# Experts' weighted rows added to their tokens in PSUM by matmuls with a selection matrix; norm read from there; pooling mixer in float32 with narrower tiles

## What is computed

```python
# first block: every token goes to 2 of 32 experts
expert = grp[:, None] * EXPERTS_PER_GROUP + top_i        # 2 per token
weights = softmax(top_v) * p_grp
for each expert e: y[e] = (silu(gate) * up) @ w_down[e]  # gate, up = split(x_rows @ w_gate_up[e])
y = zeros.at[tok_s].add(y_buf[dest] * w_s[:, None])      # weighted sum back onto the tokens
x = layer_norm(DN_ALPHA * x + y, ln2_g, ln2_b)
# second block: 16 meta tokens in front, L = 272
h = concat([meta, x]);  a = rmsnorm(h, norm_mix[0])
# pool_mixer: 4 groups of 256 columns, windows 2, 4, 8, 16 over the positions
pooled[g] = (cs - lag) / cnt - a[..., group g]
h = h + (pooled[g] @ pool_w[g]) * pool_scale
h = h + swiglu(rmsnorm(h, norm_ffn[0]), w_gate, w_up, w_down)   # then attention and a second FFN
```

## Time and profile before

| | |
|---|---|
| median of 3 runs | 1329.99 us (1329.01 to 1331.46) |
| the profiled execution, its own time | 1331.05 us |
| its span in the trace | 1329.8 us |
| PE busy | 1216.6 us (91%), weight loads 930.0 us |
| DVE busy | 545.1 us (41%) |
| ACT busy | 482.5 us (36%) |
| POOL busy | 158.2 us (12%) |
| moved by DMA | 337.38 MB, 253 GB/s read from HBM over the span |
| DMA on the SP queue | 321.46 MB, 64.1% of the 16 engines' time |

### The profile page before, as it was taken

One profiled execution on the slowest core, in us unless ns is written; L12 is line 12 of the kernel. 1 busy time (PEld: TensorE's weight loads), 2 busy tenths in 40 slices (PEclk: granted clock), 3 DMA queues, 4 the chain that ended last, 5 costly groups with the idle time before them and its releaser, 6 DMA issues. The chain is left out here.

```text
span 1329.8 us, 19383 instructions
## 1 busy us (share of the span) xinstructions
PE 1216.6 (91%) x8290; PEld 930.0 (70%) x8290; DVE 545.1 (41%) x646; ACT 482.5 (36%) x594; POOL 158.2 (12%) x169
## 2 busy tenths in 40 slices
PE   6999999899998888888877389999999999999998
PEld 6999889744433323232322279999999998999998
DVE  5665565600110001000001676665555436666643
ACT  6544663221211111111101544444346656544432
POOL 0630000002112010101000260000120000300011
PEclk9999999699999999999999589999999999999999
DMA  9743458399999999999997845544553233455530
GB/s 335 249 144 104 169 194 322 154 367 422 422 421 422 422 422 422 422 422 421 422 421 301 258 132 164 187 155 166 177 174 127 95 128 124 161 191 190 175 112 32
DMA packets 148949, 337.38 MB, mean 254 GB/s; under 512 B 7346, under 2 KB 118107, under 8 KB 124158
## 3 DMA queue, kind: packets, MB, share of 16 engines
q1 hardware_dynamic: 143280, 321.46, 64.1%
q0 software_dynamic: 3216, 9.44, 2.0%
q10 hardware_dynamic: 2366, 5.22, 1.1%
HBM read 329.79 MB, written 6.30 MB: 253 GB/s over the span
## 5 line engine op out<-in xcount | busy, mean ns | idle before, releaser
L1523 DVE TENSOR_TENSOR lo<-raw,hi 128x2048 fp32r<-128x2048 f32 (+1 forms) x112 | 251.3, 2247 | 154.0 <-ACT hi L1092 121.4
L1092 ACT CAST hi<-raw 128x2048 fp32r<-128x2048 f32 (+1 forms) x115 | 213.5, 1858 | 115.5 <-PE PS L432 96.0
L430 PE MATMUL PS<-AH,hi 128*128 128x272 f32 (+1 forms) x832 | 238.0, 286 | 2.5 <-DVE AL L1909 2.3
L432 PE MATMUL PS<-AH,lo 128*128 128x272 f32 (+1 forms) x832 | 237.3, 285 | 0.0
L431 PE MATMUL PS<-AL,hi 128*128 128x272 f32 (+1 forms) x832 | 237.0, 285 | 0.0
L430 PEld LDWEIGHTS PS<-AH,hi 128*128 128x128 f32 x832 | 156.9, 189 | 3.6 <-DVE AL L1909 2.9
L432 PEld LDWEIGHTS PS<-AH,lo 128*128 128x128 f32 x832 | 157.0, 189 | 0.0
L431 PEld LDWEIGHTS PS<-AL,hi 128*128 128x128 f32 x832 | 156.5, 188 | 0.1
L1870 DVE TENSOR_TENSOR HM<-T,PS 64x512 f32<-64x512 f32 x32 | 22.1, 690 | 313.8 <-ACT T L1278 313.8
L1278 ACT ACTIVATE T<-PS 64x512 f32<-64x512 f32 x32 | 18.9, 590 | 237.6 <-PE PS L702 237.6
L431 PE MATMUL PS<-FL,hi 128*128 128x272 f32 (+1 forms) x352 | 100.3, 285 | 0.0
(11 more groups left out here) (389 smaller groups left out, 2133.6 us busy)
## 6 DMA issues: line engine op xcount, KB each, us to landing
raw<-in_w_gate_up_dram SPq DMA_DIRECT2D x48, 1024.0 KB, 27.0
half<-in_w_gate_up_dram SPq DMA_DIRECT2D x45, 1024.0 KB, 27.7
spare<-in_w_gate_up_dram SPq DMA_DIRECT2D x35, 1024.0 KB, 27.0
half<-in_w_down_dram SPq DMA_DIRECT2D x26, 1024.0 KB, 28.0
raw<-in_w_down_dram SPq DMA_DIRECT2D x24, 1024.0 KB, 27.8
raw<-in_ffn_w_gate_dram SPq DMA_DIRECT2D x22, 1024.0 KB, 5.2
raw<-in_ffn_w_up_dram SPq DMA_DIRECT2D x22, 1024.0 KB, 5.3
raw<-in_w_in_dram SPq DMA_DIRECT2D x21, 1024.0 KB, 7.7
```

What stands on the lines that cost most here:

```text
L430: pe.matmul(o, w(h, c), xh(k), start=start and c == 0, stop=False)
L432: r = pe.matmul(o, w(l, c), xh(k), start=False, stop=stop and c == len(ks) - 1)
L1092: act.copy(K.view(K.hi[i % HN], 0, [[1, n]]), K.view(K.rbuf[i], 0, [[1, n]])).then_inc(S.hi, 1)
L1523: r = e.tensor_tensor(K.view(K.lo[i % HN], 0, [[1, n]]), K.view(K.rbuf[i], 0, [[1, n]]), K.view(K.hi[i % HN], 0, [[1, n]]).bitcast(F32), A ...
```

## The change

**Experts.** The selection matrix now has KEEP = 40 columns for each expert, 160 for four (`GR`). A ninth gather product brings each slot's weight (SW, a float32 matmul with ones) to WS. The transposes of `turn` now go to the bank of the gate, and DVE multiplies them with the weights as it copies them to HT. After down(e) ACT rounds the two halves to YH and DVE takes the rest to YL; two experts share one pair of tiles (64 partitions each). `combine(q)` adds expert pairs to the tokens: 8 matmuls 512 wide with a selection matrix SEL that DVE makes (`pick`), into banks 0 to 3, where four float32 matmuls with ALPHA times the identity (AI) have put x*ALPHA. `d_y`, its stores and the indirect loads are gone, and POOL has nothing left to do in the stage but two memsets. DVE makes the selection matrices of all groups.

**Around the end of the stage.** ln2's gain and offset come earlier, are spread by PE behind turn(30) and turn(31) and copied by ACT (LGB), and PE waits for these copies before its warming matmuls and down(31). The pooling constants are 1152 columns in place of 2752 and are loaded together with the meta tokens once down(30) is done. A fifth `spare` slot is used six times. P0 no longer waits for the gathered rows.

**Block two.** The layer norm reads its sums from PSUM. The RMS norm isn't split. Pooling is made with float32 matmuls, 256 wide for the first half of the tokens, 128 for the second, 16 for the meta tokens; PF is evacuated by DVE and ACT and is multiplied in float32 with P0 as loaded. `rest_lo` of P0+1 and P0+2 is DVE's.

```diff
 def gather(g, ks):
-    pe.matmul(bank(b, 0, [1, 256]), view(x, 1024 * i + 256 * (k // 2) + k % 2, [[2, 128]]), view(K.SS[g % 2], 256 * i, [[1, 256]]), ...)
+    if k == 8:
+        pe.wait_ge(S.sw, g + 1)
+        for i in range(2):
+            r = pe.matmul(o, con("ones"), view(K.SW, GR * i, [[1, GR]]), start=i == 0, stop=i == 1)
+    else: pe.matmul(o, view(x, ...), view(K.SS[g % 2], GR * i, [[1, GR]]), ...)
...
 def down(e):
-    if e >= 2:
-        pe.wait_ge(S.yy, e - 1)
-        pe.wait_ge(S.y_hi, e - 1)
+    if e:
+        pe.wait_ge(S.y_lo, 2 * e)
...
+def combine(q):
+    pe.wait_ge(S.y_lo, 4 * q + 4)
+    pe.wait_ge(S.pick, q + 1)
+    for i in range(2):
+        for x in (K.YH, K.YL):
+            for c in range(2):
+                r = pe.matmul(bank(2 * i + c, 0, [1, 512]), view(K.SEL, 128 * i, [[1, 128]]), view(x, 512 * c, [[1, 512]]),
+                              start=False, stop=q == 15 and x is K.YL, skip_group_check=True)
+        r.then_inc(S.comb, 1)
...
     for e in range(NE):
         up(e)
+        if e == 2:   # x * ALPHA into banks 0 to 3
+            for i in range(2):
+                for c in range(2):
+                    pe.matmul(bank(2 * i + c, 0, [1, 512]), K.AI[:, :], view(K.X1, 1024 * i + 512 * c, [[1, 512]]), start=True, ...)
+        if e >= 3 and e % 2:
+            combine((e - 3) // 2)
         if e:
             down(e - 1)
...
-    pe.wait_ge(S.warm, 2)
-    pe_warm(pe, K, S, K.X1H, 14)
+    pe.wait_ge(S.lgb, 4)
+    pe_warm(pe, K, S, K.X1H, 14, GB)
     down(NE - 1)
+    combine(15)
...
 def store(e):   # ACT, and the rest on DVE
-    act.copy(view(K.YY, 512, [[1, 512]], rows=64), bank(DB + e % 2, 0, [1, 512], p0=64, rows=64)).then_inc(S.y_hi, 1)
+    for c in range(2):
+        act.copy(view(K.YH, 512 * c, [[1, 512]], 64 * (e % 2), 64), bank(DB, 0, [1, 512], p0=64 * c, rows=64)).then_inc(S.y_hi, 1)
...
 # pe_second
-            for x in (h, l):
-                r = pe.matmul(bank(b, 0, [1, L]), view(x, col + 128 * k, [[1, 128]], rows=rows), pmr(off, L, rows), ...)
+    def pools(i, k):
+        w = 256 - 128 * i
+        return pe.matmul(bank(4 + k // 2, 256 * (k % 2) + 128 * i, [1, w]), view(K.XR, 1024 * i + 128 * k, [[1, 128]]), pm(BANDW * (k // 2), w), ...)
...
-                pe.matmul(bank(b, 0, [1, L]), view(h, w, [[1, 128]]), hc(K.AH, 2 * g + c), ...)   # and two more
+                r = pe.matmul(bank(k % 4, 0, [1, L]), view(K.rbuf[K.P0], ...), hc(K.PF, 2 * g + c), ...)
...
 # sp_first
-    sp.wait_ge(S.rr3, 16)
     for i in range(K.P0, K.P0 + RN):
```

More of the change, by code:

```diff
@@ L134 @@
 RN, HN = 6, 3
-ONCE = 8
+SOME = [8 + 17 * i for i in range(6)]
 def weight_units(t):
@@ new lines, in pe_second @@
+    first = lambda k, c: pm(4 * BANDW + 2 * NMETA * (k // 2) + c, NMETA, NMETA)
+    meta = lambda k: view(K.XRM, 128 * k, [[1, 128]], rows=NMETA)
+    pe.wait_ge(S.pm, 16)
+    pe.wait_ge(S.rms_hi, 1)
+    pe.wait_ge(S.lgb, 4)
+    for k in range(8):
+        r = pe.matmul(bank(7, NMETA * k, [1, NMETA]), meta(k), first(k, 0), start=True, stop=True)
+    r.then_inc(S.pl_pe, 1)
+    pe.wait_ge(S.rms_hi, 2)
+    for k in range(8):
+        if k == 2:
+            pe.wait_ge(S.warm, 5)
+        elif k == 4:
+            pe.wait_ge(S.y_lo, 2 * NE)
+        elif k == 6:
+            pe.wait_ge(S.pl_dve, 1)
+        pools(0, k)
+        pe.matmul(bank(4 + k // 2, 256 * (k % 2), [1, NMETA]), meta(k), first(k, NMETA), start=False, stop=False, skip_group_check=True)
@@ L811, in pe_second @@
+    turn(1)
+    pe.wait_ge(S.rms_hi, 3)
+    for k in range(8):
+        r = pools(1, k)
+        if k % 2:
+            r.then_inc(S.pl_pe, 1)
+    loaded(pe, K, S, K.P0)
     for g in range(4):
-        pe.wait_ge(S.pl_lo, g + 1)
+        if g < 2:
+            pe.wait_ge(S.pl_dve, g + 2)
+        else:
+            pe.wait_ge(S.pl_act, g - 1)
         for m in range(2):
             k = 2 * g + m
-            b = k % 4
             if k >= 4:
@@ L1524, in rest_lo @@
                         K.view(K.hi[i % HN], 0, [[1, n]]).bitcast(F32), ALU.subtract)
-    r.then_inc(S.lop if i in K.on_pool else S.lo, 1)
+    r.then_inc(S.lo, 1)
 def dve_ahead(dve, K, S, i, end):
-    if i + 2 < end and i + 2 not in K.on_pool:
+    if i + 2 < end:
         rest_lo(dve, K, S, i + 2)
@@ new lines, in pick @@
+    def pick(q):
+        to = lambda c: view(K.DSTB, 128 * c, [[256, 2], [1, 128]])
+        two = lambda x: view(x, 0, [[128, 2], [1, 128]])
+        slot = K.con("slot", q, 1)
+        if q:
+            dve.wait_ge(S.comb, 2 * q)
+        else:
+            dve.wait_ge(S.act_step, STEP["rows"])
+        a = own(dve.tensor_scalar(two(K.SF), to(0), slot, None, ALU.is_equal))
+        own.wait(dve, a)
+        dve.scalar_tensor_tensor(two(K.SEL), to(1), slot, two(K.SF), ALU.is_equal, ALU.add).then_inc(S.pick, 1)
@@ L1882, in dve_experts @@
+    gate(0)
+    turn(0)
+    for e in range(NE):
+        g = e // 4
+        if e:
+            gate(e)
+            store(e - 1)
+            turn(e)
+        if e >= 2 and e % 2 == 0:
+            pick((e - 2) // 2)
+        if e % 4 == 0 and g + 1 < 8:
+            dve.wait_ge(S.gat, NG * g + (NG if g else 9))
+            r, _ = group_rows(dve, K, S, own, g + 1)
+            r.then_inc(S.sel, 1)
+            group_weights(dve, K, S, own, g + 1).then_inc(S.sw, 1)
+    pick(15)
     store(NE - 1)
@@ new lines, in dve_second, with factor, sums @@
+    gain, offset = (view(K.LGB, c, [[1, 1024]]) for c in (0, 1024))
+    def factor(n):
+        rows = NMETA if n == 1 else 128
+        dve_rms_factor(dve, S, own, n, *(view(K.small, 80 + 2 * n + c, [[1, 1]], rows=rows) for c in range(2)))
+    def sums(i):
+        return lambda c, w: bank(2 * i, c, [1, w])
+    nm = lambda k, n, w: view(K.pc, PC["nm"][0] + k, [[1, n], [0, w]])
+    dve.wait_ge(S.lgb, 4)
+    dve.wait_ge(S.comb, 31)
+    dve_row_norm(dve, K, S, own, 0, 3, sums(0), gain, offset)
```

582 lines of the change are left out of this document (299 added, 283 removed).

## The result

The changed kernel took 1309.76 us (median of 4 runs, 1306.70 to 1314.50) beside 1330.55 for the kernel before: ratio 0.985, 95% interval 0.981 to 0.989, about 21 us faster. I had said 1288.5. The direction was right; half of the gain did not come, and the time lies outside my range of 1280 to 1298. The profiled execution is one of the quicker ones: 1306.70, span 1305.4.

What follows compares the result with a forecast made beforehand. It took weight loads plus stores on DMA to bound the later expert stage, and PE the FFN. 13.5 - 0.5 + 0 + 28.5 = 41.5 us off 1331.05 gave 1289.5, as median 1288.5; range 1280 to 1298.

Steps and rivals of the forecast that it cites:

- Stores: Expert stage: removing 30 stores at 0.45 us each takes 13.5 us off, if the loads remain the bound.
- the loads' line: Expert stage: DMA needs 14.85 us an expert without stores, putting the last expert's silu at 700.6.
- The step that failed first: Expert stage: PE takes 13.8 us an expert, last silu at 697.0, so DMA still ends last by 3.6 us.
- the 14.1: Expert stage, sign of being wrong: middle experts over 14.1 us apart, where about 13.8 was expected.
- priced PE's waiting at 0.3: Expert stage: 0.3 us added for each gather of three, since PE needs a bank back after ScalarE's first copy.
- The end of the stage: From the last expert's silu to the last down's end: zero change, range -0.8 to +1.5 us.
- Norms: After the last down: first norm done at 9.3 us, second at 14.7 us.
- My terms for ACT: After the last down: ScalarE's copies, DMA issue, table loads, squares, split and root take 7.9 us, so ScalarE is last.
- The step that failed second: Pooling, first half: eight products of 256 columns and eight short ones take 4.4 us on PE, ending at 18.6 after the last down.
- From the FFN's first product on: FFN to the end: PE is the bound and the change leaves it alone; 538.5 us at full pace stay.
- PE bound: Rival, chance 0.18: PE becomes the bound in the expert stage; 1292 to 1298 us.
- low clock: Rival, chance 0.11: low clock holds through the transition, pooling and P0's products cost 4 to 8 us more; 1293 to 1297.

Runs made afterwards that it cites:

- store_twice: Kernel before the change, with a second 160 KB store behind each store of experts 0 to 30; 1342.48 us against 1328.00.
- gather_first: Changed kernel with ScalarE's copies of gathered tokens ahead of its copies of the expert's result; 1302.79 us.
- end_order: Changed kernel with the warming ahead of down(31) in bank 5, not waiting for LGB, and the early table load behind the LGB copies; 1308.24 us.
- meta_after: Changed kernel with the pooling's eight 16-column meta products moved from between the eight 256-column products to behind them; 1303.03 us.
- two to five: Four kernels: changed kernel with gather_first and meta_after edits; then cumulatively adding end_order, a moved spreading product, two warming fills; 1296.49, 1297.25, 1296.82, 1294.97 us.
- seven: Changed kernel with gather_first, meta_after and end_order edits, plus the meta rows' own products between the fourth and fifth wide pooling product; 1301.15 us, ratio 0.980.
- comb_double: Changed kernel with each of the first 15 combines' products done twice, 16 in place of 8; 1344.28 us.
- mid_warm: Changed kernel with 16 more warming products of 256 columns between the meta rows' first products and the pooling; 1305.61 us.

## Why the prediction was half right

1. *"Stores ... 13.5 us off everything behind the loads, if the loads remain the bound."* The price held (0.45 each in store_twice), the loads' line too (425.2 to 426.8 from silu(0)); the condition didn't. (Six units of 2.47 are 14.82, not 14.85; it changes nothing.)
2. **The step that failed first:** *"13.8 each in place of 12.34 ... So DMA still ends last, by 3.6 us"*. From silu(0) I had PE's line at 422.0; it is 433.1. Of the 11: the pace is 14.0, and the 0.2 come from the combine (2.05, not 1.9) and from gathers that cost 0.1 to 0.25 more each, about 5 over 24 experts; three falls of the clock, 1.7 each, 5.1; and 1.4 in the last three, most of it the 0.88 that up(31) waits for ScalarE; less 0.6 that I had too much up to silu(4). With the falls the middle experts lie 14.2 apart, beyond the 14.1 that I had named as the sign of being wrong. I had written that ACT's two copies now stand ahead of the gather copies, and priced PE's waiting at 0.3; by the silus it is 0.40 to 0.55. I had not seen that a wait of 0.6 amid narrow products can bring half speed for the wide ones behind it. gather_first takes wait and falls away.
3. The end of the stage: *"zero"*, found +2.0. PE is late against the loads now: its wait for ScalarE's copies ended 10.3 behind silu(31), where I had 9.5, and warming and down(31) ran partly at the low clock (7.6 together; at full about 5.4, by 3.03 for 24 warming products and 3.65 for 16 records of down). In end_order's profile the piece is 0.6 shorter; the cause is only partly shown.
4. Norms: right, and a little better than said (U + 13.4 against 14.7 for the second). My terms for ACT add up to 7.7 and not the 7.9 that I wrote; the root ended at U + 7.2.
5. **The step that failed second:** *"eight products of 256 columns and eight short ones, 4.4"*. At full clock, in a row, they take 5.5 (a product of 16 rows and 16 columns takes 0.24, not the 0.12 that my 4.4 leaves for it), alternating 7.6 by 0.95 a pair, and at the low clock they took 12.8. The second half took 3.4 for 1.75, the transposes 1.8 for 1.1. From XR to P0: 7.25 said, 8.25 in meta_after, 9.8 to 9.9 in two to five, 17.95 in the changed kernel.
6. From the FFN's first product on: as said, 542.8 to 543.0 to the end in all kernels of the changed form but end_order and seven (544.4), whose clock fell for 3.4 us early in it.

I had *PE bound* (1292 to 1298) and *low clock* (1293 to 1297) as separate rivals with 0.18 and 0.11; both came true at once, in one execution, and the low clock cost 7.6 in the transition (17.95 less 8.25, less 2.1 that the alternation costs at full clock too) and 5.1 in the stage, where I had 4 to 8 in the transition alone. What is missing in the profile: 7.0 (stage) + 2.0 (its end) + 10.8 (transition) - 2.1 (start) - 0.6 = 17.1 of the 41.5. The 2.1 of the start came by luck, else it would be 19. The median lies 3.1 above the profiled execution.

## What to carry to other kernels

Where a change takes work from the bound and gives some to its neighbour, lay the two lines side by side with their errors: a margin of 0.15 us an expert was smaller than the error of one term. Price an engine's new work together with what its order does to waits; the same copies in another order were worth 7 us, the same 16 products in another order another 6 to 7. Keep narrow products together and wide ones together, and let no short wait fall among the narrow ones.

## What the runs showed of the hardware

- PE's granted clock fell to half (1.2 GHz) not only behind long idles, but behind a gather of 160-column products with one wait of 0.59 and four small transposes; it came back while PE did wide products, each time at a cost of about 1.7 us. That befell 21 of 147 such gathers, and none of the 147 without the wait. The Trainium skill tells of the like (TensorE: Matmul & The Clock Gate, A second HAM failure mode: psum-queue depth-cycling): short idles between groups of products make the clock swing. The rows agree in part, with a fall in each of six groups in comb_double, and none in the stage of the kernel before, with its 75 short waits among wide products.
- Once the clock was down, PE alternating without any idle between one product of 256 columns and one of 16 columns kept it at 0.50 for 13.7 or 17.1 us, in six of the seven kernels that alternate. The alternation alone doesn't take it down: in mid_warm, where it was back at full behind the warming products, eight pairs but the first ran at full clock.
- A float32 product of 16 rows and 16 columns took 0.24 us among its like, and 0.32 between wide ones; a wide one between small ones 0.63 for 0.46 in a row.
- Falls differ from run to run of one kernel: the changed kernel's four runs lie at 1306.7, 1306.9, 1312.7 and 1314.5 with mean clocks 0.979, 0.979, 0.971 and 0.971.
